# Reordering the second mixer of a two-block network: projections, levels, convolutions, state space, heads and rows

## What is computed

```python
def hybrid_layer(x, ...):
    u = rms_norm(x, attn_norm_w) @ w_in
    hq, hf, hi, hg, aq, ak, av, sz, sxbc, sdt = jnp.split(u, points, axis=-1)
    mix = jnp.concatenate([
        hgrn2_mixer(hq, hf, hi, hg, lower_bound, hgrn_norm_w),
        dilated_attention_mixer(aq, ak, av, q_norm_w, k_norm_w, rel_bias),
        mamba2_mixer(sz, sxbc, sdt, ssm_conv_w, ssm_conv_b, ssm_dt_bias, ssm_a_log, ssm_d, ssm_norm_w),
    ], axis=-1)
    x = x + mix @ w_out
    return x + peer_ffn(rms_norm(x, ffn_norm_w), ...)
```

## Time and profile before

| | |
|---|---|
| median of 3 runs | 2506.33 us (2505.19 to 2507.14) |
| the profiled execution | 2506.24 us, span 2504.4 us |
| PE busy | 2420.6 us, 97% of the span |
| DVE busy | 1802.3 us, 72% |
| ACT busy | 1254.9 us, 50% |
| POOL busy | 381.0 us, 15% |
| first of the two second mixers: pair's end to end of the heads | 600.07 to 735.66 us |
| second of them | 1554.71 to 1694.61 us |
| rows of w_out behind them | 22.48 us |

### The profile page before, as it was taken

The page is one execution under the profiler, slowest core; times in us unless marked ns, Lnnn a source line. Parts: engine busy times, 40 slices in busy tenths (PEclk is TensorE's granted clock), DMA queues, the critical chain, the costliest instruction groups (busy, mean ns, idle before and its releaser), DMA issues.

```text
span 2504.4 us, 39135 instructions
## 1 busy us (share of the span) xinstructions
PE 2420.6 (97%) x15670; PEld 2108.7 (84%) x15670; DVE 1802.3 (72%) x3442; ACT 1254.9 (50%) x1793; POOL 381.0 (15%) x310
## 2 busy tenths in 40 slices
PE   7999798999999999999999999899999999999999
PEld 7987778988888888888888887888888888888887
DVE  8787946656645778888887555754777888988555
ACT  3544545445555565555444545454565555444444
POOL 3023321002433610000000001340730000000000
PEclk9999999999999999999999999899999999999999
DMA  9696524555224454444445555324455444454554
GB/s 389 206 367 221 197 102 167 215 199 177 102 102 171 174 191 175 170 169 166 180 174 207 187 199 185 111 102 154 169 185 185 169 169 170 169 183 169 213 189 151
DMA packets 73029, 455.77 MB, mean 182 GB/s; under 512 B 9099, under 2 KB 15371, under 8 KB 20754
## 3 DMA queue, kind: packets, MB, share of 16 engines
q1 hardware_dynamic: 72162, 452.21, 50.1%
q0 software_dynamic: 688, 1.06, 0.3%
HBM read 449.17 MB, written 4.06 MB: 181 GB/s over the span
## 4 chain that ended last, share of the span: by engine, by line
PE 85%; DVE 9%; ACT 3%; POOL 1%; issue 1%; DMA 0%; SPq 0%; DVEq 0%; POOLq 0%; ACTq 0%
PE ps L379 19%; PE ps L352 16%; PE ps L353 16%; PE ps L354 16%; PE ps L381 8%; PE ps L2527 2%; DVE wlo L334 2%; PE ps L398 1%; PE ps L378 1%; DVE raw L345 1%; ACT whi L315 1%; DVE XB L1207 1%; ACT xn L475 1%; PE ps L1137 1%; PE ps L2507 1%
## 5 line engine op out<-in xcount | busy, mean ns | idle before, releaser
L315 ACT ACTIVATE whi<-raw 128x1024 fp32r<-128x1024 f32 x765 | 809.8, 1060 | 1050.7 <-PE ps L354 645.0
L334 DVE TENSOR_TENSOR wlo<-raw,whi 128x1024 fp32r<-128x1024 f32 x657 | 806.3, 1230 | 497.3 <-ACT whi L315 496.9
L379 PE MATMUL ps<-HT,whi 128*128 128x512 f32 x2048 | 718.7, 399 | 0.0
L381 PE MATMUL ps<-HT,wlo 128*128 128x256 f32 x1792 | 502.1, 280 | 0.0
L379 PEld LDWEIGHTS ps<-HT,whi 128*128 128x128 f32 x2048 | 372.3, 188 | 68.9
L352 PE MATMUL ps<-whi,CT 128*128 128x512 f32 x1024 | 404.0, 395 | 1.5 <-DVE wlo L334 1.1
L353 PE MATMUL ps<-wlo,CT 128*128 128x512 f32 x1024 | 398.7, 389 | 0.0
L354 PE MATMUL ps<-whi,CT 128*128 128x512 f32 x1024 | 398.6, 389 | 0.0
L381 PEld LDWEIGHTS ps<-HT,wlo 128*128 128x128 f32 x1792 | 338.6, 189 | 8.6
L334 POOL TENSOR_TENSOR wlo<-raw,whi 128x1024 fp32r<-128x1024 f32 x108 | 264.7, 2453 | 341.7 <-ACT whi L315 341.7
L352 PE MATMUL ps<-HT,whi 128*128 128x256 f32 x968 | 280.8, 290 | 7.5 <-DVE wlo L334 4.2
(11 more groups left out here) (393 smaller groups left out, 3317.8 us busy)
## 6 DMA issues: line engine op xcount, KB each, us to landing
raw<-in_down SPq DMA_DIRECT2D x128, 1024.0 KB, 4.9
raw<-in_up SPq DMA_DIRECT2D x128, 1024.0 KB, 4.8
raw<-in_w_in SPq DMA_DIRECT2D x41, 1024.0 KB, 4.9
raw<-in_ffn_gu SPq DMA_DIRECT2D x36, 1024.0 KB, 4.9
raw<-in_w_ada SPq DMA_DIRECT2D x28, 1024.0 KB, 6.4
raw<-in_ffn_d SPq DMA_DIRECT2D x22, 1024.0 KB, 5.9
raw<-in_w_out SPq DMA_DIRECT2D x12, 1024.0 KB, 4.9
raw<-in_w_ada SPq DMA_DIRECT2D x16, 512.0 KB, 12.9
```

What stands on the lines that cost most here:

```text
L315: e.activation(self.whi[:, i % NSPLIT, :], self.raw_of(i), ACT.Copy, bias=0.0, scale=1.0).then_inc(*k.inc("w_hi", ("hi", i)))
L334: e.tensor_tensor(self.wlo[:, n, :], self.raw_of(i), self.whi[:, n, :].bitcast(F32), ALU.subtract).then_inc(*k.inc("w_lo_pool" if pool els ...
L379: t = e.matmul(out.rearrange("p (a t) -> p a t", a=2), hi[:, s], self.HT[:, c, :, :], start=c == 0, stop=c == 7)
L381: t = e.matmul(out[:, 0:T], lo[:, s], self.HH[:, c, :], start=False, stop=False)
```

## The change

In both second mixers:

- The token tiles come in the order q and k (three), z1, z with a part of v, v0, i, g; z is evicted plainly and gets its silu as a whole in round 21. The weights in `lay` are laid out in this order. `QKT` has three buffers instead of two.
- Levels stand in a table: level 0 in round 3, levels 1 to 8 in rounds 3, 5, 7, 9, 11, 12, 13, 14 (the round in which the exponentials are made; products one round later, copies two later). Their PSUM banks are a table as well: levels 6, 7, 8 all use banks 2 and 3. On DVE a round now begins with copies and sums of the levels, and the low part and the convolution follow; on ACT the exponentials come ahead of the high part.
- The first tap of a convolution is ACT's, at the eviction, straight from PSUM; DVE does the other three a round later.
- The state space part begins a round or two earlier; its gating and norm are done for both groups at once, in rounds 22 to 24.
- Heads begin in round 20, one a round without gaps; their turning uses bank 3. The states of hgrn2 stand in round 25 and use bank 0, their output in rounds 26 to 29.
- There are 32 rounds; rows slots 0 to 4 stand in rounds 27 to 31, ahead of the heads' and output's steps of the round. The order of the chunks is 5, 6, 7, 2, 3, 4, 0, 1.
- None of a second mixer's low parts is POOL's.

The core of the diff:

```diff
-for _s in (165, 465):
-    ON_POOL |= set(range(_s + 2, _s + 31, 2))
...
-        return [(h, r - t.first_head - h - h // 3) for h in range(t.n_heads) if 0 <= r - t.first_head - h - h // 3 < 4]
+        return [(h, r - t.first_head - h - h // t.group) for h in range(t.n_heads)
+                if 0 <= r - t.first_head - h - h // t.group < 4]
...
-        t.Q, t.K, t.V, t.B, t.score, t.turn, t.out, t.mh = t.QN, t.KN, t.AV, (t.B0, t.B1), (4, 5), 7, 2, 2
-        t.n_heads, t.first_head, t.hides = 6, 26, False
+        t.Q, t.K, t.V, t.B, t.score, t.turn, t.out, t.mh = t.QN, t.KN, t.AV, (t.B0, t.B1), (4, 5), 3, 2, 2
+        t.n_heads, t.first_head, t.hides, t.group = 6, 20, False, 6
...
-        t.toks = ("z1", "z", "g", "qk0", "qk1", "qk2", "i", "v0")
-        t.rounds = 36
+        t.toks = ("qk0", "qk1", "qk2", "z1", "z", "v0", "i", "g")
+
+        t.levels = {3: 1, 5: 2, 7: 3, 9: 4, 11: 5, 12: 6, 13: 7, 14: 8}
+        t.product_bank = (2, 6, 2, 6, 2, 6, 2, 2, 2)
+
+        t.rows, t.rounds = 27, 32
...
         def hgrn(r):
-            if 4 <= r < 13:
-                products(r - 4)
-            if r == 28:
+            if r == 3:
+                products(0)
+            if r - 1 in t.levels:
+                products(t.levels[r - 1])
+            if r == 25:
...
+        rows = (tag, t.out_slot, t.MH, t.ML, (5, 6, 7, 2, 3, 4, 0, 1), lambda c: [(tag, "mh", c), (tag, "ml", c)], (4, 5, 6, 7))
         for r in range(t.rounds):
-            proj(r)
+            if r < t.rows:
+                proj(r)
+            else:
+                self.rows_main(e, *rows, r - t.rows)
             hgrn(r)
             mamba(r)
-            if r in (21, 23, 25):
-                turn_qk((r - 21) // 2)
+            if r in (17, 18, 19):
+                turn_qk(r - 17)
             for h, seg in self.heads_at(r, t):
                 self.head_pe(e, t, h, seg)
-            if r == 26:
+            if r == 25:
...
-            if r == 31:
+            if r == 29:
                 out([(j, 128 * j, j) for j in range(2)], [(tag, "mix0")])
-        rows = (tag, t.out_slot, t.MH, t.ML, (5, 6, 7, 0, 1, 2, 3, 4), lambda c: [(tag, "mh", c), (tag, "ml", c)], (4, 5, 6, 7))
-        for j in range(5):
-            self.rows_main(e, *rows, j)
...
                 if name == "xr":
+                    for w in k.late(("used", i), ("c2", l)):
+                        e.wait_ge(*w)
+                    e.activation(t.XB[:, c, :], PS[:, b, 0:T], ACT.Identity, bias=self.vec2(l, "conv_b")[:, c:c + 1],
+                                 scale=self.vec2(l, "conv_w")[:, 21 + c:22 + c]).then_inc(*k.inc("act_proj", (tag, "xc", c, 3)))
                     evict((tag, "xr", c), [("used", i)], t.XR[:, c, :], PS[:, b, 0:T])
...
+            if r == 21:
+                for w in k.late((tag, "z"), (tag, "z1")):
+                    e.wait_ge(*w)
+                e.activation(t.SZ[:, :, :], t.SZ[:, :, :], ACT.Silu, bias=0.0, scale=1.0).then_inc(*k.inc("act_mamba", (tag, "sz")))
...
         for r in range(t.rounds):
-            proj(r)
+            if r == 4:
+                products(0)
+            if t.levels.get(r - 2, 8) < 8:
+                products(t.levels[r - 2])
+            if r in t.levels:
+                decays(t.levels[r])
+            if r < t.rows:
+                proj(r)
+            else:
+                self.lo(e, t.out_slot + r - t.rows + 3)
             hgrn(r)
             mamba(r)
             attn(r)
```

More of the change, by code:

```diff
@@ L1195, in head_dve, with conv_dve @@
                                 ALU.mult).then_inc(*k.inc("dve_head", (t.tag, "dg", h, tt)))
-    def conv_dve(self, e, what, need, out, src, w, b):
+    def conv_dve(self, e, what, need, out, src, w, b=None):
         k = self.k
-        for x in k.late(*need):
-            e.wait_ge(*x)
-        e.tensor_scalar(out, src, w(3), b, ALU.mult, ALU.add).then_inc(*k.inc("dve_conv", (*what, 3)))
+        if b is not None:
+            for x in k.late(*need):
+                e.wait_ge(*x)
+            e.tensor_scalar(out, src, w(3), b, ALU.mult, ALU.add).then_inc(*k.inc("dve_conv", (*what, 3)))
         for j in (2, 1, 0):
             n = 3 - j
-            for x in k.late((*what, j + 1)):
+            for x in k.late((*what, j + 1), *need):
                 e.wait_ge(*x)
@@ L1238, in mixer1_tiles @@
         t.Q, t.K, t.B, t.score, t.turn, t.out, t.mh = t.QT, t.KT, (t.B0, t.B1), (2, 3), 6, 7, 0
-        t.n_heads, t.first_head, t.hides = 8, 18, True
+        t.n_heads, t.first_head, t.hides, t.group = 8, 18, True, 3
         t.qk_ready = lambda c: [("mix1", "q", c), ("mix1", "k", c)]
@@ L1895, in hgrn @@
         def hgrn(r):
-            if 4 <= r < 13:
-                products(r - 4)
-            if r == 28:
-                for w in k.late((tag, "at", 7, 0), (tag, "at", 7, 1), (tag, "at", 8, 0), (tag, "at", 8, 1), (tag, "i"), *self.free[6]):
+            if r == 3:
[3 more added lines that the diff above has]
+            if r == 25:
+                for w in k.late((tag, "at", 7, 0), (tag, "at", 7, 1), (tag, "at", 8, 0), (tag, "at", 8, 1), (tag, "i"), *self.free[0]):
                     e.wait_ge(*w)
@@ L2052, in proj @@
                 if name in ("qk0", "qk1", "qk2"):
-                    c = t.toks.index(name) - 3
-                    two = lambda x: x[:, c % 2, :].rearrange("p (a n) -> p a n", a=2)
-                    evict((tag, "qsq", c), need + ([(tag, "qs", c - 2)] if c > 1 else []), two(t.QSQ), src, ACT.Square)
-                    evict((tag, name), need + ([(tag, "qk turned", c - 2)] if c > 1 else []), two(t.QKT), src)
+                    c = t.toks.index(name)
+                    two = lambda x: x.rearrange("p (a n) -> p a n", a=2)
+                    evict((tag, "qsq", c), need + ([(tag, "qs", c - 2)] if c > 1 else []), two(t.QSQ[:, c % 2, :]), src, ACT.Square)
+                    evict((tag, name), need, two(t.QKT[:, c, :]), src)
                 if name == "i":
@@ L2078, in hgrn @@
                 e.activation(t.PF[:, :], t.FG[:, :], ACT.Ln, bias=0.0, scale=1.0).then_inc(*k.inc("act_hgrn", (tag, "pf", 0)))
-            if r == 12:
+            if t.levels.get(r - 2) == 8:
                 for par in range(2):
@@ L2153, in mixer2_act @@
         for r in range(t.rounds):
-            proj(r)
+            if r in t.levels:
[3 more added lines that the diff above has]
+            else:
+                self.hi(e, t.out_slot + r - t.rows + 3)
             hgrn(r)
             mamba(r)
-            if r in (21, 23, 25):
-                copies((r - 21) // 2)
+            if r in (17, 18, 19):
+                copies(r - 17)
             attn(r)
-            if r == 26:
-                out([(5 + j, (0, 1, 3)[j]) for j in range(3)])
-            if r == 31:
+            if r == 25:
+                out([(5 + j, (7, 6, 4)[j]) for j in range(3)])
+            if r == 29:
                 out([(j, j) for j in range(2)])
-        for j in range(5):
-            self.hi(e, t.out_slot + j + 3)
         self.close_act(e, n + 1, t.out_slot + 8, [("used", t.slot + 27)])
@@ L2402, in mamba @@
                                     ALU.mult).then_inc(*k.inc("pool_mamba", (tag, "skip", tt)))
-            if r in (21, 24):
-                g = (r - 21) // 3
-                self.rstd_pool(e, (tag, "ms", g), [(tag, "ms", g, 1)], t.ms[:, g, 2:4], t.ms[:, g, 0:2], 2, 192)
+            if r == 23:
+                for g in range(2):
+                    self.rstd_pool(e, (tag, "ms", g), [(tag, "ms", g, 1)], t.ms[:, g, 2:4], t.ms[:, g, 0:2], 2, 192)
         for r in range(t.rounds):
-            if r < 27:
-                self.lo(e, t.slot + 4 + r, True)
-            if r == 28:
+            self.lo(e, t.slot + 4 + r, True)
+            if r == 27:
                 eight = lambda x: x.rearrange("p a (h d) -> p (a h) d", d=64)
```

145 lines of the change are left out of this document (69 added, 76 removed).

## The result

| | before | after |
|---|---|---|
| median | 2506.33 us (3 runs; 2506.10 with a fourth) | 2488.05 us (2484.04 to 2491.39, 4 runs) |
| ratio | | 0.9925, interval 0.9911 to 0.9939 |
| the profiled execution, span | 2504.4 us | 2489.6 us |
| first of the second mixers, norm to norm | 171.13 us | 164.58 us |
| second of them, norm to norm | 174.60 us | 164.95 us |

The changed kernel is 18 us faster where 28.7 had been forecast. 2488.05 us lies on the upper edge of the range, 2473 to 2488, and well outside 2474 to 2482, to which the forecast had given a chance of 0.60. "Norm to norm" is from the first transpose of the norm ahead of a mixer (PE, L520) to the one behind its rows.

What follows compares the result with a forecast made beforehand. PE, busy 97% of the span, bounds the kernel, so only its waits and low clock can go: 20.98 + 1.84 + 0.83 + 8.04 = 31.69 us, less 3.0, gives 28.7 and 2477.5 us; range 2474 to 2482, with rivals 2473 to 2488.

Steps and rivals of the forecast that it cites:

- The level rounds: Five level rounds in each second mixer: waits and half clock lose 20.98 us together, all to be had.
- the tie's 0.3 us: Level rounds: DVE delivers levels 2 to 6 about when PE asks, some 0.3 us lost in all.
- the loss of 8.76: First mixer's five level rounds, 31.71 against 22.95 us undisturbed; said to be nearly all DVE time blocked by POOL's low parts.
- The turning of x: State space part: turning a round earlier removes PE's wait before the first decay, 0.92 us a mixer, 1.84 in both.
- The table loads: Three more on ACT a mixer, 1.28 us each; costed at nothing given a 3.6 us lead, 0.8 without it.
- The last heads: Heads at the mixers' end: idle time from the unfilled PE, DVE, ACT chain goes, 8.04 us in both mixers.
- the start: First four slots of the second of the mixers, 12.52 against 11.69 us: 0.83 us gained, bounds 0 and 1.6.
- (a): Level rounds: small POOL work blocks DVE too, one 2.30 us power per mixer, 2482 us; chance 0.05.
- (b): DVE stays the bound of the level rounds: 2486 us, chance 0.11; with a clock fall 2491, chance 0.09.
- (c): Last heads still paced by their chain, behind high and low parts: 8.04 us comes back, 2485.5; chance 0.07.
- (d): State space rounds: DVE's waits hold up low parts beyond their lead, 24 us a mixer, 2523 us; chance 0.04.
- (e): No gain: PE's lost time turns up elsewhere in the mixer, within 5 us of 2506; chance 0.02.

Runs made afterwards that it cites:

- both repairs: Changed kernel with NC evicted on DVE in round 13 instead of 14 and ACT's squares behind the head's steps in round 22; 2477.10 us, again 2477.83 us.

## Why the prediction was right, and where it was wrong

**The level rounds: right in the walk, wrong about the cause.** The forecast walked both queues from the end of the pair, which came 1.53 us later in after. Levels 2 to 6 were to be asked for at 621.3, 628.8, 636.4, 643.9 and 648.5; less 1.53, the products start at 621.5, 629.2, 636.7, 644.2 and 648.8. Of the tie's 0.3 us, 0.2 showed. DVE's pair of rounds was put at 7.5 to 8.0 us and took 7.33. The wait for banks at level 7, 0.9 us, did not show.

"So the loss of 8.76 is nearly the blocked time alone" does not hold. Taking GpSimd's low parts away alone brings back about half of the loss. Windows of PE from level 1's products to level 7's in the first mixer, six rounds of 4.59 or 27.54 us when undisturbed, in the kernel before and in the one without low parts on GpSimd:

```profile
616.67:652.98 36.31, 31.67 (x241) 0.86 0.24 88
```

```profile
618.75:651.31 32.56, 30.66 (x242) 0.90 0.28 98
```

8.8 us lost become 5.0; in the second mixer 36.72 us become 31.77, 9.2 lost become 4.2. The forecast counted four blocked operations and some 8 us. In the five rounds of the 31.71 us window there are three, of 2.64, 2.67 and 2.00 us at 629.32, 636.65 and 649.72, and they are 5.9 us over their usual 0.48, 0.48 and 0.43; and each low part that moves to DVE costs it 1.2 us there. In after only 0.2 us of waits is left there, so the other half came from the rest of the change. Spreading the levels was not the needed part: with the first tap on ACT, they can stand in a row. The first tap is worth 6.7 us by itself; in the text it was 0.4 us in a sum of 7.5. The new order within a round, sums ahead of the low part, was not tried alone, so its share stays open.

**The turning of x: the step that failed.** "The turning is now a round earlier, with level 8's products in between, and the wait goes." The wait for the evicted x went (the 1.58 us window of the earlier trace rows is 0.76 now), but the turning itself got a wait of 2.2 us. I had looked at who uses the turned x and not at who holds the bank it goes into. The diff moves the turning on PE from round 16 to 14 and the sums from 14 to 13, and leaves `NC` on DVE in round 14, behind that round's low part. So a wait that the sum put at nothing cost 4.9 us a mixer, more than half of it in clock, while of the 1.84 some 1.6 did come. Moving `NC` by a round gave 9.2 us back in the mixers. The forecast had named the sign itself, "or if a clock below 1.0 stands there": it stands there at 0.50, and from the pair's end to the end of the rows the mixers took 152.11 and 152.81 us where about 146 was expected.

**The table loads: costed at nothing, and not nothing.** The lead of 3.6 us counted slots for the low part alone. It holds for low parts: PE never waits more than 0.2 us for one. It does not hold for what stands behind a late high part in ACT's and DVE's queues and has no lead: the gated product, the squares, the first head's probabilities. 1.6 us a mixer; 2.9 in both came back with the squares behind the head, and 1.7 with the silu left out.

**The last heads: right; the start: mostly not.** No wait is left behind the first head. The rows slots between heads are 0.1 to 0.3 us longer, which the sum did not have. What the slots are worth was not measured in the order before. At the start the three slots from the pair's end to level 0's products take 9.65 us in the second mixer against 9.05 in the first: its loss is 0.6 instead of 0.83, so only a quarter of that small term came.

**The rivals.** (a), small operations of POOL block DVE: out. The taps of after are all 0.47 to 0.48 us, and nine of the 21 in each mixer overlap operations of POOL's softplus. The Trainium skill, "SBUF — State Buffer", section "Who interferes with whom", would have them contend too; here the 128x1024 low parts did and the 128x12 operations did not. (b), DVE the bound: not in the levels, though with the first tap back it is at once. (c), heads paced by their chain: only the first head waits, 1.5 us a mixer, and behind the squares, not behind high and low parts. (d): out; PE waits 0.2 us for low parts. (e), the gain not there at all: no, but what it named, lost time that turns up elsewhere in the mixer, took 28.7 - 18.3 = 10.4 us by the medians.

The order that the forecast described, in which no new wait stands between levels and heads, is the kernel with both repairs: 2477.1 and 2477.8 us against 2477.5. The stretches that the sum named did give up their loss; the reading of the order was not complete, and the reason given for the largest term was half right. That the two agree to 0.4 us is partly luck, since terms of 0.8 to 1 us came out differently in both directions. That the changed kernel itself landed on the edge of the range is luck too: the range reached to 2488 for other reasons, a slower DVE in the level rounds or heads paced by their chain, and neither of these is what came.

## What to carry to other kernels

When a change moves a step on one engine, follow the PSUM bank and every other buffer it writes back to the last reader, and look where that reader stands in its own queue; a copy left behind a low part cost 3.6 to 5.1 us a mixer where the earlier step was to save 0.9. A lead in buffers protects only the work that goes through those buffers, not the small operations queued behind it. Of two engines with nearly equal rounds, count the lead and the number of rounds before you call one the bound, and take a helper away from the queue alone before you reorder anything around it.

## What the runs showed of the hardware

- A low part of 128x1024 on POOL stretched DVE's operation beside it to 2.0 to 2.68 us, five times in each mixer up to the state space: taps with two inputs, the first tap `XB<-XR,c` with one tensor and a column of factors as input (2.41 us instead of 0.41), a `QK` from two buffers, and an update of `PF` from `PF` alone. Most of them ended 0.28 us after the low part. DVE's products `MA<-EX,ps`, which read one input from PSUM, took their usual 0.55 us beside a low part. Taps beside operations of 128x12 on POOL, of 0.2 to 2.30 us, were not stretched. Size is not all or nothing: beside a POOL operation of 128x512 (`HG`, 1.10 us) in the kernel before, a `DG` took 0.64 us instead of 0.28.
- The length of a wait alone does not tell whether the clock falls, nor for how long. After 2.19 and 1.43 us at the turning of x, PE had been granted 0.50 at once; after 1.53 us for `PT` it stayed at 1.00. After 0.70 us for `QK` it fell in the kernel with low parts on GpSimd, and after 1.06 and 0.69 us for `QK` in the same rounds with the first tap on DVE it did not. Windows of PE, the two slots behind such a wait and its products, first with low parts on GpSimd (0.70 us of wait), then with the tap on DVE (1.06 us):

```profile
639.86:647.29 7.43, 7.43 (x49) 0.77 0.42 143
```

```profile
633.89:640.60 6.71, 6.02 (x50) 1.00 0.45 156
```

  In the second mixer of the latter, the same execution and the same instructions, the clock did fall behind the wait of 0.69 us:

```profile
1587.26:1594.70 7.44, 7.44 (x50) 0.77 0.40 141
```

  What tells them apart stays open; the price of a wait can only be given as a range.
- A stage that no edit touched, 219.5 to 386 us, took 166.06 to 168.21 us in profiles of the same kernel, so a difference of 2 us between two spans says nothing about an edit.
